# Modulation chunks of a conformer and attention block moved into the loops of two MLPs, three in each round

## What is computed

```python
def second_block(x, c, ada_w, ada_b, ...):
    cond = jax.nn.silu(c)
    for i in range(DEPTH_2):                      # DEPTH_2 = 2
        mod = cond @ ada_w[i] + ada_b[i]          # 1024 x 6144 for each layer
        sh1, sc1, g1, sh2, sc2, g2 = [m[:, None, :] for m in jnp.split(mod, N_MOD, axis=-1)]
        h = rms_norm_2(x, mix_norm_g[i]) * (1.0 + sc1) + sh1
        ...                                       # y: convolution (i = 0) or attention (i = 1)
        x = x + g1 * y
        h = rms_norm_2(x, mlp_norm_g[i]) * (1.0 + sc2) + sh2
        x = x + g2 * (jnp.square(jax.nn.relu(h @ mlp_w1[i])) @ mlp_w2[i])
    return x
```

## Time and profile before

| | us |
|---|---|
| median of 3 runs | 1109.22 |
| the profiled execution, its own time | 1110.23 |
| its span in the profile | 1108.4 |
| TensorE busy, matmuls | 1053.7 (95%) |
| VectorE busy | 709.8 (64%) |
| ScalarE busy | 491.9 (44%) |
| GpSimd busy | 133.4 (12%) |
| DMA: 221.6 MB, mean | 200 GB/s |
| first MLP | 232 to 415 |
| second MLP | 558 to 748 |
| QKV of the attention layer | 756 to 854 |
| third MLP | 920 to 1104 |

### The profile page before, as it was taken

The page is one execution under the profiler, slowest core; times in us unless marked ns, Lnnn a source line. Parts: engine busy times, 40 slices in busy tenths (PEclk is TensorE's granted clock), DMA queues, the critical chain, the costliest instruction groups (busy, mean ns, idle before and its releaser), DMA issues.

```text
span 1108.4 us, 16827 instructions
## 1 busy us (share of the span) xinstructions
PE 1053.7 (95%) x6872; PEld 928.2 (84%) x6872; DVE 709.8 (64%) x831; ACT 491.9 (44%) x554; POOL 133.4 (12%) x74
## 2 busy tenths in 40 slices
PE   6999998999999999998999999998978799999998
PEld 6997776899999989976799999986856489989996
DVE  4868556687667687433696777668784748454463
ACT  5345536444344445432544433445324835444441
POOL 0030002010010040022011000001132501100000
PEclk9999999999999999999999999999889999999999
DMA  8884335738787753657258877863664324656540
GB/s 287 301 303 141 125 114 173 269 113 313 265 289 270 271 163 118 181 146 245 76 188 307 271 259 269 300 228 114 229 230 150 114 77 137 197 170 200 187 172 38
DMA packets 119740, 221.58 MB, mean 200 GB/s; under 512 B 6338, under 2 KB 20740, under 8 KB 119684
## 3 DMA queue, kind: packets, MB, share of 16 engines
q1 hardware_dynamic: 119056, 219.17, 58.5%
q0 software_dynamic: 432, 1.57, 0.5%
q10 hardware_dynamic: 196, 0.05, 0.0%
HBM read 215.07 MB, written 1.05 MB: 195 GB/s over the span
## 4 chain that ended last, share of the span: by engine, by line
PE 80%; DVE 10%; ACT 5%; issue 3%; DMA 1%; SPq 1%; ACTq 0%; POOL 0%; DVEq 0%
PE ps L417 75%; DVE ada_acc L869 2%; ACT hi L347 2%; PE ps L855 2%; PE ps L454 1%; PE ps L731 1%; DVE lo L358 1%; PE ps L657 1%; DMA raw<-in_w_in 0%; DVE hTl L504 0%; ACT aS L1592 0%; DVE stat L1890 0%; ACT gate L1491 0%; DMA prow<-in_c 0%; DVE aS L1885 0%
## 5 line engine op out<-in xcount | busy, mean ns | idle before, releaser
L358 DVE TENSOR_TENSOR lo<-raw,hi 128x2048 fp32r<-128x2048 f32 x147 | 345.7, 2357 | 273.2 <-ACT hi L347 272.7
L347 ACT ACTIVATE hi<-raw 128x2048 fp32r<-128x2048 f32 x153 | 292.4, 1913 | 348.7 <-PE ps L417 335.1
L417 PE MATMUL ps<-hTh,hi 128*128 128x256 f32 x992 | 282.7, 285 | 2.0 <-DVE hTl L504 1.9
L417 PE MATMUL ps<-hTh,lo 128*128 128x256 f32 x992 | 280.7, 283 | 0.0
L417 PE MATMUL ps<-hTl,hi 128*128 128x256 f32 x992 | 280.7, 283 | 0.0
L417 PEld LDWEIGHTS ps<-hTh,hi 128*128 128x128 f32 x992 | 190.3, 192 | 3.8 <-DVE hTl L504 2.5
L417 PEld LDWEIGHTS ps<-hTl,hi 128*128 128x128 f32 x992 | 190.3, 192 | 0.3
L417 PEld LDWEIGHTS ps<-hTh,lo 128*128 128x128 f32 x992 | 190.3, 192 | 0.0
L417 PE MATMUL ps<-hi,hidh 128*128 128x512 f32 x416 | 162.8, 391 | 0.4 <-DVEq L652 0.4
L417 PE MATMUL ps<-hi,hidl 128*128 128x512 f32 x416 | 162.1, 390 | 0.0
L417 PE MATMUL ps<-lo,hidh 128*128 128x512 f32 x416 | 162.0, 389 | 0.0
(11 more groups left out here) (216 smaller groups left out, 909.3 us busy)
## 6 DMA issues: line engine op xcount, KB each, us to landing
raw<-in_mlp_w SPq DMA_DIRECT2D x64, 1024.0 KB, 5.3
ada_raw<-in_ada_w SPq DMA_DIRECT2D x48, 1024.0 KB, 7.3
raw<-in_w_in SPq DMA_DIRECT2D x21, 1024.0 KB, 7.3
raw<-in_w_ff_in SPq DMA_DIRECT2D x16, 1024.0 KB, 5.4
raw<-in_w_ff_out SPq DMA_DIRECT2D x16, 1024.0 KB, 6.8
raw<-in_attn_w_qkv SPq DMA_DIRECT2D x12, 1024.0 KB, 6.3
raw<-in_conv_w_in SPq DMA_DIRECT2D x8, 1024.0 KB, 5.6
taps<-u_pad SPq DMA_DIRECT2D x64, 71.0 KB, 2.8
```

Source lines behind the costliest of these rows:

```text
L347: nc.scalar.activation(hi[:, slot], raw[:, slot], ACT.Copy).then_inc(hi_made, 1)
L358: nc.vector.tensor_tensor(lo[:, slot], raw[:, slot], hi[:, slot].bitcast(F32), ALU.subtract).then_inc(lo_made, 1)
L417: return nc.tensor.matmul(o, lhs, rhs, start=start, stop=False, skip_group_check=True)
```

## The change

No chunk is computed in the first stage or in the QKV any more. The loops of the first two MLPs take three in each round, so that each of the two has 11 chunks with head and tail (before: 8); the third MLP keeps its two. The three chunks of a round have an accumulator each; the two new ones lie in the area `big`, where `y_tmp` is used by the norms. The tables ADA_STEPS, ADA_LOADS and ADA_KEEPS say at which j of a round a half is computed, loaded, and a chunk kept: the halves at j = 0, 2, 3, 4, 5, 6, the keeps at 4, 6, 7. The sums stand behind u+3, u+5 and u+7. With the chunks go their loads, their waits, and ScalarE's and GpSimd's waits for them in the first stage.

```diff
--- before.py
+++ after.py
@@ -150,7 +150,7 @@
         hidl = hid_area("hidl", 8192, [P, 8, SEQ], F32R)
 
         ada_raw = ada_area("ada_raw", 0, [P, 2, 4, 512])
-        ada_acc = acc_area("ada_acc", 0, [P, 512])
+        ada_acc = [acc_area("ada_acc0", 0, [P, 512])]
         pool_mean = acc_area("pool_mean", 0, [P, 2, SEQ])
         row_a = row_area("row_a", 0, [P, D])
         row_b = row_area("row_b", 4096, [P, D])
...
@@ -160,6 +160,7 @@
         junk_act = big("junk_act", 1024, [P, TT, 2, 512])
         junk_dve = big("junk_dve", 9216, [P, 512])
         y_tmp = big("y_tmp", 12288, [P, D])
+        ada_acc += [big("ada_acc1", 12288, [P, 512]), big("ada_acc2", 14336, [P, 512])]
         relu = big("relu", 16384, [P, 4 * SEQ])
...
-            pe.wait_ge(ada_kept, (10, 18, 18, 24)[2 * layer + i] + 1)
+            pe.wait_ge(ada_kept, (11, 22, 22, 24)[2 * layer + i] + 1)
...
-            ada_sum(pe, ADA_HEAD[m][0])
+            ada_sum(pe, ADA_HEAD[m])
...
+
+            def loop_sum(q, i):
+                if m < 2:
+                    ada_sum(pe, ada_loop(m, i)[q])
 
             def second(par_, u, j, chunk, after=(None, None), final=False):
                 pe.wait_ge(hid_lo, chunk)
@@ -771,16 +776,15 @@
                 n, s = 8 * i + (u0 + 2), u0 + 2
                 first(1, n, s, 2 * i + (8 * m + 1))
                 second(0, n + 2, s + 2, 2 * i + (8 * m + 1))
-                if m < 2:
-                    ada_sum(pe, ada_loop(m, i)[0][0])
+                loop_sum(0, i)
                 first(2, n + 4, s + 4, 2 * i + (8 * m + 2))
+                loop_sum(1, i)
                 second(1, n + 6, s + 6, 2 * i + (8 * m + 2))
-                if m < 2:
-                    ada_sum(pe, ada_loop(m, i)[1][0])
+                loop_sum(2, i)
...
-                   (lambda: ada_sum(pe, ADA_TAIL[m][0]), (lambda: gate_row(pe, m - 1, 1)) if m else None))
+                   (lambda: ada_sum(pe, ADA_TAIL[m]), (lambda: gate_row(pe, m - 1, 1)) if m else None))
...
-        ADA_IN = [(0, 0, 6), (1, 0, 7)]
-        ADA_QKV = [(18 + q, 1, 6 + q) for q in range(4)]
-
-        ADA_HEAD = ((2, 0, 8), (10, 0, 10), (22, 1, 10))
-        ADA_TAIL = ((9, 0, 9), (17, 0, 11), (23, 1, 11))
+        ADA_HEAD = ((0, 0, 0, 2), (11, 0, 11, 2), (22, 1, 10, 2))
+        ADA_TAIL = ((10, 0, 10, 0), (21, 1, 9, 0), (23, 1, 11, 0))
+
+        ADA_STEPS = {0: (0, 0), 2: (0, 1), 3: (1, 0), 4: (1, 1), 5: (2, 0), 6: (2, 1)}
+        ADA_LOADS = {1: (0, 0), 2: (0, 1), 4: (1, 0), 6: (1, 1), 7: (2, 0), 8: (2, 1)}
+        ADA_KEEPS = {4: 0, 6: 1, 7: 2}
 
         def ada_loop(m, i):
 
-            return [(2 * i + (8 * m + 3 + q), m, 2 * i + q) for q in range(2)]
+            return [(3 * i + (11 * m + 1 + q), m, 3 * i + (1 - m + q), q) for q in range(3)]
 
         def ada_load(sp, chunk, h):
 
-            number, layer, c = chunk
+            number, layer, c, _ = chunk
...
-        def ada_sum(pe, number):
-
+        def ada_sum(pe, chunk):
+
+            number, acc = chunk[0], ada_acc[chunk[3]]
             pe.wait_ge(ada_step, number * 8 + 16)
             pe.wait_ge(ada_kept, number + 1)
             for q in range(4):
-                last = nc.tensor.matmul(ps[:, 6, q:q + 1], ada_acc[:, q * P:(q + 1) * P],
+                last = nc.tensor.matmul(ps[:, 6, q:q + 1], acc[:, q * P:(q + 1) * P],
                                         ones[:, 0:1], start=True, stop=True)
             last.then_inc(ada_cols, 1)
...
-        def ada_unit(dve, number, h):
-
+        def ada_unit(dve, chunk, h):
+
+            number, acc = chunk[0], ada_acc[chunk[3]]
             dve.wait_ge(ada_landed[h], number * 16 + 16)
             for k in range(4):
                 step = number * 8 + (8 + 4 * h + k)
                 w, s = ada_raw[:, h, k], cond[:, 4 * h + k:4 * h + k + 1]
                 if h == 0 and k == 0:
-                    ins = nc.vector.tensor_scalar(ada_acc[:], w, s, None, ALU.mult)
+                    ins = nc.vector.tensor_scalar(acc[:], w, s, None, ALU.mult)
...
-                    if ada is not None and j % 2 == 0:
-                        ada_unit(dve, ada[j // 4][0], j // 2 % 2)
+                    if ada is not None and j in ADA_STEPS:
+                        q, h = ADA_STEPS[j]
+                        ada_unit(dve, ada[q], h)
                     dve_step(dve, u + j, j=s + j)
                     if j % 4 == 1:
                         lo_of(1 - j // 4, chunk + j // 4)
-                    if ada is not None and j in (3, 7):
-                        ada_keep(dve, ada[j // 7])
+                    if ada is not None and j in ADA_KEEPS:
+                        ada_keep(dve, ada[ADA_KEEPS[j]])
...
-                for j in range(8):
-                    c = 2 * i + (2, 1, 3, 2)[j // 2]
-                    (first, second)[j // 2 % 2](n + j, s + j, c, j % 2)
-                    if m < 2 and j % 2 == 0:
-                        ada_load(sp, ada_loop(m, i)[j // 4], j // 2 % 2)
+                for j in range(9):
+                    if j < 8:
+                        c = 2 * i + (2, 1, 3, 2)[j // 2]
+                        (first, second)[j // 2 % 2](n + j, s + j, c, j % 2)
+                    if m < 2 and j in ADA_LOADS:
+                        q, h = ADA_LOADS[j]
+                        ada_load(sp, ada_loop(m, i)[q], h)
...
-                    elif 2 * c + h >= 5:
-                        half = 2 * c + h - 5
-                        ada_load(sp, ADA_IN[half // 2], half % 2)
             load(sp, U_GV, win[:, :, 2048:2304])
-            ada_load(sp, ADA_IN[1], 1)
...
-                    if 2 <= c:
-                        ada_load(sp, ADA_QKV[c - 2], h)
...
-                if h == 0:
-                    ada_sum(pe, 0)
...
-            ada_sum(pe, 1)
...
-                ada_sum(pe, ADA_QKV[0][0])
-                pe.wait_ge(ada_kept, 18 + 2)
                 gate_row(pe, 1, 0)
 
             qkv(0)
             qkv(1, first_unit_done)
             pe.wait_ge(row_kept, 3)
-            qkv(2, lambda: ada_sum(pe, ADA_QKV[1][0]))
-            qkv(3, lambda: ada_sum(pe, ADA_QKV[2][0]))
-            qkv(4, lambda: ada_sum(pe, ADA_QKV[3][0]))
-            pe.wait_ge(ada_kept, 22 + 1)
+            qkv(2)
+            qkv(3)
+            qkv(4)
...
-            act.wait_ge(ada_step, 8 + 8 * 2)
...
-                if u in (2, 3, 5, 6):
-                    ada_unit(dve, *((0, 0), (0, 1), (), (1, 0), (1, 1))[u - 2])
...
-                if 1 <= c < 5:
-                    ada_keep(dve, ADA_QKV[c - 1])
                 dve_step(dve, U_QKV + 2 * c, turn=c > 0)
-                if c < 4:
-                    for h in range(2):
-                        ada_unit(dve, ADA_QKV[c][0], h)
...
-            pool.wait_ge(ada_kept, 2 + 1)
```

More of the change, by code:

```diff
@@ L865, in ada_unit @@
                 if h == 0 and k == 0:
-                    ins = nc.vector.tensor_scalar(ada_acc[:], w, s, None, ALU.mult)
+                    ins = nc.vector.tensor_scalar(acc[:], w, s, None, ALU.mult)
                 else:
                     dve.wait_ge(ada_step, step)
-                    ins = nc.vector.scalar_tensor_tensor(out=ada_acc[:], in0=w, scalar=s, in1=ada_acc[:],
+                    ins = nc.vector.scalar_tensor_tensor(out=acc[:], in0=w, scalar=s, in1=acc[:],
                                                          op0=ALU.mult, op1=ALU.add)
@@ L876, in late_steps @@
                 if chunk is not None:
-                    ada_unit(dve, chunk[0], h)
+                    ada_unit(dve, chunk, h)
                 dve_step(dve, last - 1 + h)
         def ada_keep(dve, chunk):
-            number, layer, c = chunk
+            number, layer, c, _ = chunk
             dve.wait_ge(ada_cols, number + 1)
@@ L914, in mlp_dve @@
                 if j < 2:
-                    ada_unit(dve, ADA_TAIL[m][0], j)
+                    ada_unit(dve, ADA_TAIL[m], j)
                 dve_step(dve, u0 + 26 + j)
@@ L1635, in _ @@
                                             ALU.mult).then_inc(par_ok, 1)
-                if u == 4:
-                    ada_keep(dve, ADA_IN[0])
                 if u == 3:
@@ L1641, in _ @@
                                           pair(2).rearrange("p b n -> p (b n)")).then_inc(kT_kept, 1)
-            ada_keep(dve, ADA_IN[1])
             def gelu(i, x, dst):
```

## The result

The changed kernel takes 1116.88 us, the median of 4 runs (1115.53 to 1117.97), the kernel before 1108.86 us in the same comparison: 8.0 us more, a ratio of 1.0073 with a 95% interval of 1.0061 to 1.0085. It is slower, by about twice the 3.8 us that were forecast.

A forecast was written before the change was run, and what follows sets the result against it. TensorE was taken to bound the kernel, busy 1053.7 of 1108.4 us. Costs of 27.5 us less gains of 23.7 gave +3.8, 1114.0 us profiled, 1113.0 median; own range 1111.5 to 1117, 8 in 10 from 1100 to 1121.

The forecast's parts named there:

- second wait: MLP rounds, third sum: TensorE waits 1.4 us for the second chunk's keep; rival without this wait 1103 us.
- QKV: Two modulation waits, the slow clock behind them and four sums leave the QKV: 21.7 us gained.
- First stage: Two sums leave the first stage, one with its wait and step to the next unit: 2.0 us gained.
- its units there follow without a pause: First stage: leaving loads and ScalarE's wait cost TensorE nothing, so no gain was counted for them.
- First wait: MLP rounds, second sum: TensorE waits 1.9 us for the first chunk's keep, behind a load landing 7.3 us after issue.
- The gentler rival: MLP rounds: load lands 6.2 us after issue, first wait 0.8 us, total 1106.4 us; chance 0.08.
- no loss: MLP loops: TensorE's clock costs nothing behind waits of 1.9 and 1.4 us, as whole units lie between waits.
- the fall behind each first wait: Rival, MLP loops: the clock falls behind each first wait, up to 1125 us; chance 0.12.
- the bound of 3.4 us a round: MLP rounds, upper bound: one slow stretch of 3.4 us, less the second wait it hides, 2.0 us, or +12 us.
- a clock below 1.00 in the loops: Sign in the changed profile, loops of the first two MLPs, that would show the forecast wrong.
- The row that was relied on, 836 to 838 us: Profile window, TensorE busy 0.55 of 2.0 us, clock 1.00: taken to show short halts leave the clock alone.
- the gains' side: QKV and first stage together: 23.7 us gained.

The follow-up runs named there:

- e3_gain_only: Changed kernel without computing the six moved chunks, MLP loops in their old order; 1087.37 us, ratio 0.9811 to the kernel before.
- e1: Changed kernel with the load of the second chunk's second half moved ahead of one weight load; 1123.83 us, ratio 1.0128 to the kernel before.
- e9: e6 with the first chunk's keep placed behind the third chunk's first half, so TensorE must wait for it; 1113.43 us, ratio 1.0041 to the kernel before.
- e2: Changed kernel with the first chunk's keep at j = 3 instead of 4, the load left late; 1125.76 us, ratio 1.0151 to the kernel before.
- e6: Changed kernel, one bank, two loads sooner and the second chunk's keep at j = 5 instead of 6; 1092.57 us, ratio 0.9855 to the kernel before.
- e7: Changed kernel, one bank, two loads sooner, keeps left where they are; 1095.29 us, ratio 0.9873 to the kernel before.
- e4_two_banks: Changed kernel with each round's second sum writing PSUM bank 7 instead of 6, loads left late; 1101.15 us, ratio 0.9932 to the kernel before.
- e8_keeps_alone: Changed kernel, one bank, keeps of first and second chunk at j = 3 and 5, loads left late; 1098.94 us, ratio 0.9924 to the kernel before.
- e10: e6 with the first chunk's keep placed later still than in e9, behind the lo split of j = 5; 1143.28 us, ratio 1.0305 to the kernel before.
- e5: Changed kernel with the two banks of e4_two_banks and two loads sooner; 1092.37 us, ratio 0.9856 to the kernel before.

## Why the prediction was right, and where it was not

**Direction and range.** Slower by over 0.3% had the chance 0.53, and 1116.9 us lies in the range to 1121. It lies just inside the forecast's own range, 1111.5 to 1117, whose sum came to half of what was measured. That the time lies there is in part luck: two errors of nearly 10 us each, told under the second wait, cancelled.

**QKV.** Forecast 21.7 us, measured 20.6. No wait for modulation, clock 1.00 through the projections, units of weights ready. What the forecast did not count: the transposes of Q had waited twice, 0.67 us for a keep and then 1.73 for qT. The first wait has gone, the second is now 2.62 us, and the clock fell behind it (7.11 us for the next unit, 5.51 before). e3_gain_only, where this stage takes the same 72.2 us as in the change (from its first unit), confirms it.

**First stage.** Forecast 2.0 us, measured 2.0, and this is luck. 0.8 us of it came before any chunk: 32 matmuls at the start of the launch took 5.37 us for 6.14, and they take 4.9 to 6.4 us in the twelve traces here, all with the same code there. The two sums, with the idle time around them, gave 2.3 us. But 1.9 us went into a halt that the kernel before did not have (chain, start us, us; "issue" is time for which the profile shows no releaser):

```profile
70.45 1.96 issue
```

By the program (L1195) TensorE waits there for VectorE's first GELU product (L1641). It ends at 72.31 us, 1.2 us earlier than before, and 0.8 of that is the start of the launch. Another halt, of 1.18 us at 86.68 us in the kernel before, has gone, and 0.3 us were lost to the lower clock near 200 us, where it lasted a little further into the units. So "its units there follow without a pause" was a wrong reading of the trace. The 1.5 us in the attention, which the change does not touch, are of the clock too: from the transposes to the third MLP the twelve traces here take 69.6 to 71.2 us.

**First wait.** Forecast 1.9 us a round, by a landing 7.3 us after issue, VectorE idle for 3.1 us, the keep behind a lo split. Measured 1.82, 1.71, 1.75 and 1.90 us in the later rounds, 2.88 and 2.60 in the first of each MLP, with the idle piece of 3.18 us in its place. The first rounds wait longer because their load is later still: the six loads in question took 7.1 to 7.2 us in the later rounds, 8.29 and 7.95 us in the first ones (chain, start us, us, what).

```profile
267.53 8.29 DMA ada_raw<-in_ada_w
```

The gentler rival, the load 6.2 us after issue, is out. That was the estimate from the Trainium skill, "DMA: Bandwidth & Descriptors", section "Anatomy of one DMA". The page gives the figures there for a DMA issued by GpSimd, while these loads are issued by SP, so they were no rule for this queue; the seven loads looked at behind a weight load (six here, one in e1) took 7.1 us or more.

**Clock.** This is the step that failed. The text took "no loss", and gave the fall behind each first wait a chance of 0.12. It fell in all six rounds and cost 1.6 us each, 9.6 us together, about half of the bound of 3.4 us a round. One of the text's own signs of being wrong, "a clock below 1.00 in the loops", came. The Trainium skill, "TensorE: Matmul & The Clock Gate", section "HAM oscillation — how this bites in real kernels", reckons the loss as half of the time spent at the lower rate. The trace agrees: some 3.4 us at 0.50, 1.6 us lost. The row that was relied on, 836 to 838 us, lies within a halt of 1.73 us and does not reach its end at 838.27; the clock did stay at 1.00 behind it (5.51 us for the next unit), but this was one of a kind that goes either way: e9 shows both with one halt of 1.41 us. And whole units between two waits, the text's reason for "no loss", did not keep the clock up.

**Second wait.** Forecast 1.4 us a round, and 0.25 us on its sum; measured none. The mechanism holds, as e1 and e2 show by making it appear. The forecast let TensorE leave the first wait at full clock. At half clock it came 1.6 us later, at 346.27 us in the second round, and found the keep of 345.35 us done, as the bound for the clock had said ("the second wait that it hides"). Without these 1.6 us it would have stood there for about 0.8 us (an estimate from the two times). Two errors of 9.6 and 9.9 us thus nearly cancelled, and the forecast of the MLPs was 27.5 us where 29.3 were measured.

**The rest.** 3.8 us forecast against 6.4 between the profiles: +1.8 in the MLPs (the two longer first rounds and the broken overlap), -0.4 on the gains' side (1.1 less in the QKV, 1.5 more in the attention), and +1.3 in the convolution layer, which the change does not touch. There a halt of 3.4 us, in both kernels, was followed by a longer slow stretch in the changed one (0.58 in 543 to 546 us, where the kernel before had 0.98 in 530 to 533 us). The twelve traces, with the same code there, take 125.1 to 126.6 us for it. So this part is chance as far as these traces tell. Why the difference is 8.0 us in the medians and 6.4 in the profiles stays open.

**GpSimd and VectorE.** The two engines excluded each other as forecast: a multiplication of 0.48 us on VectorE took 2.04 us while GpSimd's square ran. The Trainium skill, "SBUF — State Buffer", "SBUF: two separate sides", calls it an exclusive lock held for the whole instruction; the row agrees. It adds some 1.6 us to VectorE's lateness in a round, in the change as in e1. But it does so only where VectorE is late already: in e6 and e7 the square falls almost wholly into VectorE's idle time and costs it under 0.1 us.

## What to carry to other kernels

When work is moved into a tight loop, follow every step that is issued in order (loads and small read-outs alike) to its consumer, and move each as far forward as its buffer allows: here two loads and one keep placed better (e6_order_alone) turned +8.0 us into -16.6 with the same arithmetic. An engine that is late by 3 us in a round will make someone wait somewhere; taking away the one wait that the profile shows only shifts it, and may land it where it costs more, so mend the lateness first. And price a halt of TensorE with the lower clock behind it as well: of the 31 halts of 1.15 us or more in the loops of these traces, 29 had it, of 18 halts of 0.28 to 1.06 us one. A number that comes out right, like the 2.0 us of the first stage, is no proof of the reading behind it: compare the two traces place by place.

## What the hardware showed that was not expected

TensorE's clock behind a halt in these loops: at 1.00 behind nearly all halts of 0.28 to 1.06 us, lower behind one of 0.90 (e4_two_banks) and one of 1.15 (e8_keeps_alone), both ways at 1.41, and lower behind every one of 1.71 us or more. It stayed low for 3.4 us in each round of the change as made, for 3.4 or 6.8 us, six times each, in e1 and e2, and for up to 10.2 us around the long halts of e10. In the QKV it is otherwise. The halt of 1.71 us before the transposes of K left the clock at 1.00 in every kernel here. The halt of 2.62 us before those of Q, the same in all eleven kernels without chunks there, left it at 1.00 in three (e5, e6, e10) and brought it down in eight. The 4 us behind it in e6, then in e9 (busy us of PE, PEld, DVE, ACT, POOL; PEclk; DMA share; GB/s):

```profile
820.70:824.70 4.00, 4.00 (x21) 3.33 (x22) 0.29 (x1) 1.79 (x3) 3.57 (x1) 1.00 0.63 185
...
842.18:846.18 4.00, 4.00 (x15) 3.25 (x16) 0.29 (x1) 1.85 (x3) 3.57 (x1) 0.63 0.63 189
```

That alone is 1.6 us between two kernels with the same code there (70.6 us for the stage in e6, 72.2 in e9). So a halt's length alone does not tell, nor does its place in the program, and one execution is a sample. The spread of e9_halt_short, 10 us between its runs, is of the size of such falls (six of 1.6 us); that they are its cause is not shown, since one run of it was profiled.

A second bank of PSUM was worth nothing beside the right order (e5 against e6: 0.2 us), although the wait that the profile shows is for columns of that one bank.
